# Two attention mixers with the steps of their heads in other slots

## What is computed

```python
def _even_mixer(h, w_in, ...):
    aq, ak, av, bq, bk, bv, iq, ik, iw = _split_cols(h @ w_in, EVEN_SIZES)
    ...
    ya = _diff_attention(aq, ak, av, lam, _alibi_slopes(A_HEADS))      # 4 heads, two softmaxes each
    ya = _rms_norm(ya, subln_a) * (1.0 - lam_init)
    ...
    yb = _dsa_attention(bq, bk, bv, iq, ik, iw, _alibi_slopes(B_HEADS), topk)   # 8 heads, 64 chosen keys
    return jnp.concatenate([ya.reshape(b, s, -1), yb.reshape(b, s, -1)], axis=-1)

def _odd_mixer(h, w_in, qn_c, kn_c, sinks):
    q, k, v = _split_cols(h @ w_in, ODD_SIZES)
    ...
    return _swa_sink_attention(q, k, v, sinks, _alibi_slopes(C_HEADS))  # 16 heads, window 128

x = x + g1 * (y @ w_out[l])
```

## Time and profile before

| | us |
|---|---|
| median of 3 runs (1293.46 to 1297.28) | 1296.5 |
| the profiled execution's own time | 1294.27 |
| its span | 1292.9 |
| TensorE busy in the span | 1211.4 |
| VectorE, ScalarE, GpSimd busy | 926.4, 660.2, 72.6 |
| even mixer with its output product (stretch 627 to 790): TensorE busy | 134.6 of 163 |
| odd mixer with its output product (993 to 1101): TensorE busy | 90.7 of 108 |

### The profile page before, as it was taken

How to read it: one execution, slowest core, us unless ns; L and a number is a source line. 1 busy time by engine, 2 the same in 40 slices (tenths; PEclk the granted TensorE clock), 3 DMA queues, 4 the chain that set the end, 5 groups by cost and what they waited for, 6 DMA issues and landing times.

```text
span 1292.9 us, 24807 instructions
## 1 busy us (share of the span) xinstructions
PE 1211.4 (94%) x9924; PEld 1147.9 (89%) x9924; DVE 926.4 (72%) x1753; ACT 660.2 (51%) x1144; POOL 72.6 (6%) x82
## 2 busy tenths in 40 slices
PE   5998999999998999999988789999999879999999
PEld 5877999999987999999977668999989767999999
DVE  5637698878686888879796658888875555776652
ACT  6327554444446544446555656444444766544441
POOL 1001000001000100003000101000010112000000
PEclk9999999999999999999998989999999989999999
DMA  8852698778753687788533326887875423555561
GB/s 281 239 153 83 204 305 263 253 257 279 246 176 132 212 265 255 244 276 270 197 111 100 110 87 193 270 255 253 270 242 184 135 91 105 183 185 180 181 194 66
DMA packets 81126, 258.10 MB, mean 200 GB/s; under 512 B 8872, under 2 KB 22004, under 8 KB 81012
## 3 DMA queue, kind: packets, MB, share of 16 engines
q1 hardware_dynamic: 75252, 250.69, 59.3%
q10 hardware_dynamic: 5760, 5.83, 1.9%
HBM read 253.82 MB, written 2.67 MB: 198 GB/s over the span
## 4 chain that ended last, share of the span: by engine, by line
PE 74%; DVE 14%; ACT 6%; issue 4%; POOL 1%; DMA 1%; SPq 0%; DVEq 0%; ACTq 0%; POOLq 0%
PE ps L519 66%; DVE wlo L1232 4%; PE ps L570 2%; DVE HL L1238 1%; DVE X L1238 1%; DVE aacc L1238 1%; ACT HH L845 1%; ACT oS L845 1%; ACT eS L845 1%; PE ps L626 1%; PE ps L618 1%; ACT tmp L845 1%; DVE tmp L1546 1%; PE ps L617 1%; PE ps L622 1%
## 5 line engine op out<-in xcount | busy, mean ns | idle before, releaser
L519 PE MATMUL ps<-HH,whi 128*128 128x256 f32 (+1 forms) x2152 | 624.4, 290 | 24.9 <-DVE wlo L1232 11.9
L519 PE MATMUL ps<-HH,wlo 128*128 128x256 f32 (+1 forms) x2152 | 613.9, 285 | 0.0
L519 PE MATMUL ps<-HL,whi 128*128 128x256 f32 (+1 forms) x2152 | 613.3, 285 | 0.0
L845 ACT ACTIVATE whi<-raw 128x1024 fp32r<-128x1024 f32 x363 | 382.5, 1057 | 346.0 <-PE ps L519 337.3
L1232 DVE TENSOR_TENSOR wlo<-raw,whi 128x1024 fp32r<-128x1024 f32 x363 | 441.7, 1221 | 46.1 <-ACT whi L845 45.5
L519 PEld LDWEIGHTS ps<-HH,whi 128*128 128x128 f32 x2152 | 414.2, 192 | 43.0 <-issue 29.7
L519 PEld LDWEIGHTS ps<-HL,whi 128*128 128x128 f32 x2152 | 414.1, 192 | 0.4
L519 PEld LDWEIGHTS ps<-HH,wlo 128*128 128x128 f32 x2152 | 413.6, 192 | 0.0
L519 PE MATMUL ps<-GH,whi 128*128 128x256 f32 x704 | 198.2, 282 | 0.6 <-DVE bcol L1428 0.5
L519 PE MATMUL ps<-GH,wlo 128*128 128x256 f32 x704 | 197.5, 281 | 0.0
L519 PE MATMUL ps<-GL,whi 128*128 128x256 f32 x704 | 197.5, 281 | 0.0
(11 more groups left out here) (207 smaller groups left out, 939.2 us busy)
## 6 DMA issues: line engine op xcount, KB each, us to landing
raw<-wall SPq DMA_DIRECT2D x363, 512.0 KB, 4.3
araw<-ada SPq DMA_DIRECT2D x96, 512.0 KB, 4.7
UR<-uscr ACTq DMA_DIRECT2D x32, 142.0 KB, 4.3
oBB<-kbias SPq DMA_DIRECT2D x16, 192.0 KB, 2.6
aTB<-scratch SPq DMA_DIRECT2D x12, 128.0 KB
uscr<-U ACTq DMA_DIRECT2D x8, 143.5 KB, 3.7
X<-x_in SPq DMA_DIRECT2D x2, 512.0 KB, 5.7
out<-X SPq DMA_DIRECT2D x8, 128.0 KB, 2.8
```

Source lines behind the costliest of these rows:

```text
L519: ins = pe.e.matmul(o, l, r, start=(kt == p.order[0] and i == 0), stop=(kt == p.order[-1] and i == 2))
L845: ac.then_inc(ac.e.activation(o, i, func, **kw), sem)
```

## The change

`AFTER_E` and `AFTER_O` were made by the helpers `chain`, `by_slot`, `differ`, `sparse` and `attend`; now they are written out as tables. `AFTER_D` and `BEFORE_D`, of the dilated attention, hold what they held. All else in the file is the same, on lines that are lower by 12 from there on. Every step is still there once. These change their slot or their place in it:

| mixer | step | slot before | slot after |
|---|---|---|---|
| even | dscore 0, dexp 0, dfact 0, dturn 0, dweigh 0, dnorm 0 | 20 to 25, behind top or pick | 20 to 25, ahead of it |
| even | sweigh 0, sscore 1 | 32 | 33 |
| even | sexp 1; dweigh 1, sfact 1; dnorm 1 | 33; 34; 35 | 34; 35; 36 |
| even | dout 1, sturn 2; sturn 3; sweigh 1 | 36; 37; 38 | 37; 38; 39 |
| even | dscore 3; dexp 3 | 44; 45 | 45; 46 |
| even | sexp 3; sfact 3 | 47; 48 | 48; 49 |
| even | sturn 6; sturn 7; sweigh 3 | 50; 51; 52 | 51; 52; 53 |
| odd | score 0; exp 0; fact 0 | 8; 9; 10 | 7; 8; 9 |
| odd | turn 0, score 2; turn 1, exp 2 | 12; 13 | 11; 12 |
| odd | weigh 0, fact 2 | 14 | 13 |
| odd | turn 4, score 3; turn 5, exp 3; fact 3 | 16; 17; 18 | 15; 16; 17 |
| odd | weigh 2 | 18 | 20 |
| odd | turn 6; turn 7, exp 4; weigh 3 | 20; 21; 22 | 19; 20; 21 |
| odd | exp 5; fact 5 | 23; 24 | 22; 23 |
| odd | turn 12; turn 13 | 27; 28 | 28; 29 |
| odd | weigh 6, turns 14 and 15; weigh 7 | 29; 30 | 30; 31 |

```diff
-AFTER_O = by_slot(
-    [(3, "const", 0)] + attend(0, 8) + attend(1, 10) + attend(2, 12) + attend(3, 16) + attend(4, 20, (4, 5), 7)
...
+AFTER_O = {
+    3: [("const", 0)], 7: [("score", 0)], 8: [("exp", 0)], 9: [("fact", 0)], 10: [("score", 1)],
...
```

More of the change, by code:

```diff
@@ L178 @@
 TURN_AT = {FFN_SLOTS[FFN_SLOTS.index(k) + 1]: b for k, b in SUM_AT.items()}
[L182 to L185, removed]
@@ L192, in chain @@
[L192 to L211, removed]
@@ L214, in attend @@
[L214 to L222, removed]
@@ L223 @@
-AFTER_O = by_slot(
-    [(3, "const", 0)] + attend(0, 8) + attend(1, 10) + attend(2, 12) + attend(3, 16) + attend(4, 20, (4, 5), 7)
-    + attend(5, 22) + attend(6, 24, (3, 4), 5) + attend(7, 26, (3, 3), 4))
+AFTER_D = {
+    6: [("score", 0)], 7: [("score", 1), ("exp", 0)], 8: [("log", 0), ("exp", 1)],
+    9: [("share", 0), ("log", 1)], 10: [("turn", 0), ("share", 1)], 11: [("turn", 1)],
+    12: [("score", 2), ("score", 3)], 14: [("exp", 2), ("exp", 3), ("log", 2)],
+    16: [("weigh", 0), ("share", 2), ("log", 3)]}
@@ new lines @@
+BEFORE_D = {
+    0: [("weigh", 1), ("turn", 2), ("share", 3)], 4: [("turn", 3), ("weigh", 2)], 1: [("weigh", 3)]}
+AFTER_E = {
+    3: [("const", 0)], 13: [("gain", 0), ("index", 0)], 14: [("index", 1)], 15: [("index", 2)],
+    16: [("index", 3)], 17: [("top", 0)], 18: [("top", 1)], 19: [("top", 2)], 20: [("dscore", 0), ("top", 3)],
+    21: [("dexp", 0), ("top", 4)], 22: [("dfact", 0), ("top", 5)], 23: [("dturn", 0), ("top", 6)],
+    24: [("dweigh", 0), ("top", 7)], 25: [("dnorm", 0), ("pick", 0)], 26: [("dout", 0), ("sscore", 0)],
+    27: [("sexp", 0)], 28: [("sfact", 0)], 30: [("sturn", 0), ("dscore", 1)], 31: [("sturn", 1), ("dexp", 1)],
+    32: [("dfact", 1)], 33: [("sweigh", 0), ("dturn", 1), ("sscore", 1)], 34: [("sexp", 1)],
+    35: [("dweigh", 1), ("sfact", 1)], 36: [("dnorm", 1)], 37: [("dout", 1), ("sturn", 2)],
+    38: [("sturn", 3), ("dscore", 2)], 39: [("sweigh", 1), ("dexp", 2)], 40: [("dfact", 2), ("sscore", 2)],
+    41: [("dturn", 2), ("sexp", 2)], 42: [("sfact", 2)], 44: [("sturn", 4)], 45: [("sturn", 5), ("dscore", 3)],
+    46: [("dweigh", 2), ("dfact", 3), ("dexp", 3), ("sscore", 3)], 47: [("dnorm", 2), ("dturn", 3)],
+    48: [("dout", 2), ("sweigh", 2), ("sexp", 3)], 49: [("dweigh", 3), ("sfact", 3)], 50: [("dnorm", 3)],
+    51: [("dout", 3), ("sturn", 6)], 52: [("sturn", 7)], 53: [("sweigh", 3)]}
@@ new lines @@
+AFTER_O = {
+    3: [("const", 0)], 7: [("score", 0)], 8: [("exp", 0)], 9: [("fact", 0)], 10: [("score", 1)],
+    11: [("turn", 0), ("exp", 1), ("score", 2)], 12: [("turn", 1), ("fact", 1), ("exp", 2)],
+    13: [("weigh", 0), ("fact", 2)], 14: [("turn", 2)], 15: [("turn", 3), ("turn", 4), ("score", 3)],
+    16: [("weigh", 1), ("turn", 5), ("exp", 3)], 17: [("fact", 3)], 19: [("turn", 6)],
+    20: [("weigh", 2), ("turn", 7), ("exp", 4), ("score", 4)], 21: [("weigh", 3)],
+    22: [("fact", 4), ("exp", 5), ("score", 5)], 23: [("fact", 5)], 24: [("turn", 8), ("score", 6)],
+    25: [("turn", 9), ("exp", 6)], 26: [("turn", 10), ("fact", 6), ("score", 7)],
+    27: [("weigh", 4), ("turn", 11), ("exp", 7)], 28: [("weigh", 5), ("turn", 12), ("fact", 7)],
+    29: [("turn", 13)], 30: [("weigh", 6), ("turn", 14), ("turn", 15)], 31: [("weigh", 7)]}
```

## The result

| | before | after |
|---|---|---|
| median of 4 runs each, us | 1294.98 (1292.34 to 1297.28) | 1282.44 (1279.32 to 1284.32) |
| ratio, 95% interval | | 0.9896 (0.9875 to 0.9916) |
| span of the profiled execution, us | 1292.9 | 1281.2 |

The change takes 12.5 us off, where 12.9 were forecast. The page of the changed kernel, against the earlier trace rows: busy times by engine, and the engines of the chain that ended last.

A forecast was written before the change was run, and what follows sets the result against it. A slot-by-slot walk at 2.4 GHz took the mixers to be bound by hand-offs between four fixed-order queues. Terms -10.2 + 0.4 - 3.3 - 2.3 + 2.5 = -12.9 on 1294.3, plus 2.2 to the median: 1283.5 us, range 1277.5 to 1291.5.

The forecast's parts named there:

- the clock term: Both mixers: new waits bring two stretches at 1.2 GHz, 1.25 us each; +2.5 us, bounds 0 and +7.
- Odd, start: Odd mixer, score 0 one slot earlier: TensorE stands about 1.5 us for its query; cost about zero after score 2.
- Odd, middle: Odd slots 17 to 20: fact 3 no longer behind weigh 2, turn 6 8.0 us earlier; part of the odd -10.2.
- Odd, tail: Odd turns 12 to 15, weighs 6 and 7 later: exp 7 gains about 1.2 us, last contraction step waits about 1.0.
- The products of GpSimd: Odd mixer: fact 1's products, now followed by a weight split, taken at +0.2 us, bounds 0 and 1.1.
- Even, slots 20 to 25: Head 0's steps ahead of top: turn 0's wait shrinks 0.9 us, VectorE's later work is 0.45 later; +0.4 us.
- Slots 32 to 39: Even mixer: dweigh 1's 3.48 us wait goes, a new one of about 2.7 stands at dnorm 1; -3.3 us.
- Slots 44 to 53: Even mixer: dweigh 2's 3.1 us wait goes, last contraction step waits about 1.0; -2.3 us, bounds -4 and +1.
- The second case: Whole kernel: the walk holds without the clock term, or the clock gains; 1281 down to 1276 us, chance 0.18.
- The third: Rival: only one mixer pays, 5 to 6 us stay; 1287 to 1292 us, chance 0.19.
- the fourth: Rival: nothing gained in the mixers, each removed wait comes back as another; 1293 to 1300 us, chance 0.06.
- the fifth: Rival: steps moved to tile ends lose cover, 1.45 us each for scores 0, 2, 3, turn 4; 1301 us, chance 0.07.

The follow-up runs named there:

- the filler: Changed kernel with even slots 20 to 25 in the old order, plus six idle matmuls ahead of odd scores 2 and 6: 1279.93 us, ratio 0.9888.
- even_mid: Kernel before with only slots 32 to 43 of the even mixer from the new table: 1293.76 us, ratio 0.9979.
- even_end: Kernel before with only slots 44 to 53 of the even mixer from the new table: 1294.53 us, ratio 0.9979.
- fact3_first: Kernel before with one swap in odd slot 18, fact 3 ahead of weigh 2: 1295.20 us, ratio 0.9988.
- early_undone: Changed kernel with slots 20 to 25 of the even mixer back in the old order: 1280.97 us, ratio 0.9882.
- odd_only: Kernel before with the new odd mixer table and the old even one: 1286.06 us, ratio 0.9917.
- even_only: Kernel before with the new even mixer table and the old odd one: 1290.99 us, ratio 0.9958.
- score0_late: Changed kernel with odd score 0, exp 0 and fact 0 back in slots 8, 9 and 10: 1283.67 us, ratio 0.9891.
- run 994: Not a run label: "Both run 994 matmuls" counts the even mixer's matmuls in the changed kernel and in tail_undone.
- tail_undone: Changed kernel with slots 27 to 31 of the odd mixer back in the old order: 1285.09 us, ratio 0.9910.

## Why the prediction was right

**The sum.** Forecast 1283.5, measured 1282.4. By parts of the profiled executions: even forecast -5.2 without its share of the clock term, measured -4.2; odd -10.2 likewise, measured -9.2; the clock term was +2.5. On those terms the mixers were to give -12.9 and gave -13.4. That the total comes out this close is in part luck: the terms missed by 1 us and more both ways, and the same even mixer differs by 3.1 us between two executions (last section). Of the 13.4 us TensorE's standing is 6.6 and its matmuls' own time 6.8.

**A sign of being wrong that came true for the even mixer.** The prediction named "the total of TensorE's waits in the two stretches is as before with other names". For both mixers it fell, from 45.7 to 39.1 us. For the even one alone it is as before (28.4 and 27.9). The removed waits (3.5 at dweigh 1, 2.5 of 3.1 at dweigh 2) came back as 2.2 at dnorm 1 and 0.95 at the last step, which the walk had, and as 1.45 at turn 3, 1.79 at dweigh 3 and 0.66 at a sturn, which it had not. The mixer got shorter all the same, because its matmuls ran faster. So the even terms are near in their sum and right in the waits that they name, and wrong as an account of TensorE's standing.

**Odd, start: right.** Score 0 waits 1.21 (1.5 forecast), and score 2 stands where the walk had it: the two odd mixers start 2.5 us apart (995.42 and 992.93), so 1015.09 is 1017.6 in the old counting, against 1017.4.

**Odd, middle: right mechanism, the size too large.** Turn 6 was to be 8.0 earlier and is 6.3 (1037.68 + 2.49 = 1040.2 against 1046.45), matmuls after score 4 6.5 and are 4.2, score 6 8.5 and is 6.0. The step that failed is that the walk ran at 2.4 GHz up to there. Behind score 2's wait of 1.82 twelve matmuls start 0.21 us apart instead of 0.12, and the filler, which does away with them, brings 1.3 us: the larger part of the 1.7 missing at turn 6. The prediction booked such losses apart, as the clock term. The rest (0.4, 1.0 behind score 4 and 1.2 at score 6) wasn't taken apart; turn 4's wait of 1.26 for oP and GpSimd's longer products lie on the way.

**Odd, tail: right.** The wait at the last contraction step is 0.95 (1.0 forecast), and matmuls go on at 1072.36 + 2.49 = 1074.9 in the old counting, 1.3 to 1.7 behind the walk, no more than the middle had left.

**The products of GpSimd: outside the value taken, inside the bounds.** Fact 1's pair takes 2.50 us, not 1.8, and fact 2's as much (2.72 before). Turn 2 has no wait behind it, so the slack covered it, as its bound said. A pair with a weight split beside it takes 2.50 to 2.72 us, one without 1.61, while the splits beside them keep their 1.19 to 1.23 us. At fact 1 the split starts at 1018.02 and the pair at 1018.18, so 1.0 us of the split is left, and the pair is 0.9 longer. The exclusive lock of the Trainium skill's "SBUF — State Buffer" (section "SBUF: two separate sides"), where the instruction that starts first keeps the shared ports to its end and the other is blocked, agrees with this: the pair is delayed by about what is left of the split, and the split isn't. At fact 3 the pair starts first (1035.00, the split 1035.50) and is still the one that is 1.0 longer; a pair is two instructions, and why the split doesn't wait there is open.

**Even, slots 20 to 25: +0.4 forecast, +0.7 (length) alone.** By these not told apart from nothing, nor from +1.3; at dweigh 0's start it is +0.4 in two pairs of kernels. Turn 0's wait, which was to shrink by 0.9, is 3.83 in the changed kernel against 3.17, and yet the forecast holds: the wait is 4.65 to 4.67 in four kernels with the old order there (even_mid, even_end, fact3_first, early_undone). In the kernel before turn 0 starts as far into the mixer as in three of these (48.24 us), so its TensorE was only slower to get there. The new order takes 0.8 off. It comes back at dweigh 0, which waits 1.79 us for eV instead of 0.56.

**Slots 32 to 39: -3.3 forecast, -2.0 (length) to -2.7 (ratio) alone, the term too large.** The waits are as forecast: dweigh 1's 3.48 gone, a new one at dnorm 1 of 2.22 (2.7 forecast). Part of what is missing is again the clock, half rate over the matmuls right behind that new wait, here and in even_mid (0.54):

```profile
722.60:726.00 3.40, 3.40 (x18) 3.40 (x18) 1.62 (x5) 2.43 (x6) 0.00 (x0) 0.51 0.45 154
```

**Slots 44 to 53: -2.3 forecast, -2.7 (ratio) to -3.9 (length) alone, the term too small.** Dweigh 2's wait of 3.06 is 0.57 and the 1.0 at the last step is there (0.95). The step that failed is the walk's account behind dweigh 2: it names 2.7 us at dnorm 1 as the only longer wait that stays in the even mixer, has none at turn 3 and dweigh 3, and gives the lost slow stretch no term. From dweigh 2's start to the mark the part is as long as before (44.93 and 44.69 us in even_end), with 3.1 us more standing and 3.3 less matmul time. The gain is made by dweigh 2's start, 2.5 of it by its own shorter wait.

**Clock: a loss in new places as forecast, its size shown for the odd mixer only.** The filler gives back 2.25 us in the odd mixer for two waits; the term had two at 1.25 each, over both mixers. Both were in the odd one, and the even one had its own besides, as the row above shows, so 2.5 was too little for what the term was to cover. Of the five waits of 1.5 to 2.1 us that the walk left in the odd mixer the trace has three (1.70, 1.82, 1.67). What the term left out is the other side: the slow stretches of the old order that went with its long waits, as behind dweigh 2. On balance the granted clock rose in both mixers (0.91 to 0.93, 0.94 to 0.97), and the same matmuls take 6.8 us less. How much of this the walk, at 2.4 GHz, held inside its other terms can't be taken apart. The second case was not reached: 1281 and below, measured 1282.4. By the rule quoted there from the Trainium skill ("TensorE: Matmul & The Clock Gate", Part 1) less standing means a higher clock. The odd mixer agrees, with 17.3, 11.2 and (filled) 7.9 us of standing at 0.94, 0.97 and 1.00; the even one, with the same standing at 0.91 and 0.93, doesn't show it.

**The rivals.** The third (one mixer pays) fell with odd_only and even_only, the fourth (waits come back under other names) with the lengths, the fifth with the result itself and, for score 0, with score0_late. The fourth's mechanism is real: fact3_first lost 1.7 of 3.7 us to the query right behind, and in the even mixer the waits did come back almost in full. The fifth was never near: at turn 6 the other queues had gained 6.3 us, against the 1.45 a step from which it decides.

## What to carry to other kernels

A wait that is removed from queues in a fixed order pays until the next late input, so look for the step behind it before you price it; fact 3 ahead of weigh 2 was worth at most 2.3 us alone and 5.0 with its neighbours moved, and three of the five parts tried one at a time could not be told from nothing. Count TensorE's standing and its busy time apart, too: in the even mixer the standing stayed and the same matmuls got faster. Defer whatever is behind a long run of copies on another queue if nobody needs it soon, and bring steps ahead even at the price of a short stand. And the two stands of 1.7 to 1.8 us in TensorE cost another 0.9 to 1.3 us behind them here through the clock; matmuls that nobody reads filled them and made the mixer shorter, though no run shows the whole kernel faster by it.

## What I had not expected of the hardware

The same code is not equally long from one execution to the next, and the clock goes with it. The changed kernel and the one with the odd mixer's old tail have the same even mixer, to the instruction. The row of the changed kernel stands above ("Standing or clock"); that of the one with the old tail:

```profile
629.35:791.65 162.30, 134.13 (x994) 120.50 (x993) 123.02 (x305) 96.57 (x218) 14.68 (x14) 0.96 0.40 126
```

Both run 994 matmuls, at a granted clock of 0.93 and 0.96 and with 3.1 us between them, though TensorE stands 28 us in both. That is as much as the whole term for slots 32 to 39. One piece of it can be pointed at, the matmuls behind dnorm 1's wait. In the changed kernel the clock there is 0.51, with 18 matmuls in 3.40 us (the row of 722.60); in tail_undone, behind the same wait of 2.2 us:

```profile
719.68:723.08 3.40, 3.40 (x28) 3.01 (x26) 2.04 (x6) 3.11 (x7) 0.00 (x0) 1.00 0.53 154
```

Of the eight kernels with this wait five have 0.51 to 0.54 there and three 1.00, and in the old odd mixer the wait of 1.67 us at score 2 has 1.00 behind it where the new one of 1.82 has 0.52. So a wait of about 2 us doesn't always bring a slow stretch. Ahead of the even mixer, where all fourteen kernels have the same code, it begins between 627.6 and 634.5 us, so the 3.1 us there between before and after are no effect of the change. One profile can't settle a term of 1 or 2 us in the even mixer. What makes a slow stretch fall into one execution and not into the next is open.
